# Weight panels loaded as two half transfers, each with its own semaphore

## The reference

```python
z = jnp.einsum("bsd,de->bse", n, w_in.astype(n.dtype))              # first block: mixer in
...
q = jnp.einsum("td,de->te", xt, w_q.astype(xt.dtype))               # expert router
u = expert_u[idx]
v = expert_v[idx]                                                    # 16 of 16384 experts per head and token
act = jax.nn.gelu(jnp.einsum("thkd,td->thk", u, xt))
return jnp.einsum("thk,thkd->td", (gate * act).astype(v.dtype), v)
...
def swiglu(h, w_gate, w_up, w_down):                                 # second block, four times
    return (jax.nn.silu(h @ w_gate) * (h @ w_up)) @ w_down
```

## Time and profile before

| | |
|---|---|
| time, median of 3 runs | 4292.24 us (4284.7 to 4296.47) |
| the profiled execution: its time | 4296.63 us |
| the profiled execution: its span | 4294.8 us |
| mean granted TensorE clock | 0.933 |
| PE busy | 3777.9 us, 88% of the span |
| POOL busy | 1952.1 us, 45% |
| ACT busy | 1503.3 us, 35% |
| DVE busy | 2245.2 us, 52% |
| moved by the DMA engines | 570.20 MB, mean 133 GB/s |

### The profile page before, as it was taken

How to read it: one execution, slowest core, us unless ns; L and a number is a source line. 1 busy time by engine, 2 the same in 40 slices (tenths; PEclk the granted TensorE clock), 3 DMA queues, 4 the chain that set the end, 5 groups by cost and what they waited for, 6 DMA issues and landing times. The chain is left out here.

```text
span 4294.8 us, 51143 instructions
## 1 busy us (share of the span) xinstructions
PE 3777.9 (88%) x17668; PEld 3146.6 (73%) x17668; DVE 2245.2 (52%) x3388; ACT 1503.3 (35%) x2617; POOL 1952.1 (45%) x1517
## 2 busy tenths in 40 slices
PE   6948998997888889999989884999979998469999
PEld 5526888997888889988867722788758886247887
DVE  4662696884899976663326225433243321544330
ACT  3222444663222233354322312343234422233432
POOL 3724565335666667755533300444435543004444
PEclk9978999998999999999999966999989999579999
DMA  3002344457999979733332200232313335002322
GB/s 117 15 25 83 113 157 139 147 196 283 344 334 337 338 283 352 283 98 98 93 122 62 78 0 0 85 96 91 91 59 98 97 94 106 33 1 85 97 90 91
DMA packets 172780, 570.20 MB, mean 133 GB/s; under 512 B 15457, under 2 KB 58593, under 8 KB 155140
## 3 DMA queue, kind: packets, MB, share of 16 engines
q1 hardware_dynamic: 152244, 427.68, 30.6%
q0 software_dynamic: 20432, 141.31, 9.0%
HBM read 518.85 MB, written 50.07 MB: 132 GB/s over the span
## 5 line engine op out<-in xcount | busy, mean ns | idle before, releaser
L262 POOL TENSOR_TENSOR weight_low<-weight_ring,weight_high 128x512 fp32r<-128x512 f32 x1264 | 1720.1, 1372 | 1906.1 <-ACT weight_high L234 1032.8
L277 PE MATMUL banks<-normed_high,weight_high 128*128 128x512 f32 (+1 forms) x2592 | 973.1, 375 | 118.4 <-POOL weight_low L262 115.3
L278 PE MATMUL banks<-normed_low,weight_high 128*128 128x512 f32 (+1 forms) x2592 | 962.8, 371 | 0.0
L279 PE MATMUL banks<-normed_high,weight_low 128*128 128x512 f32 (+1 forms) x2592 | 962.1, 371 | 0.0
L277 PEld LDWEIGHTS banks<-normed_high,weight_high 128*128 128x128 f32 x2592 | 494.2, 191 | 203.5 <-POOL weight_low L262 136.9
L236 ACT ACTIVATE weight_high<-weight_ring 128x512 fp32r<-128x512 f32 (+1 forms) x632 | 389.6, 616 | 673.9 <-PE banks L279 673.9
L234 ACT ACTIVATE weight_high<-weight_ring 128x512 fp32r<-128x512 f32 x632 | 398.5, 631 | 612.6 <-PE banks L279 511.4
L278 PEld LDWEIGHTS banks<-normed_low,weight_high 128*128 128x128 f32 x2592 | 494.3, 191 | 62.9 <-issue 0.5
L279 PEld LDWEIGHTS banks<-normed_high,weight_low 128*128 128x128 f32 x2592 | 493.4, 190 | 62.7
L277 PE MATMUL banks<-parked_high,weight_high 128*128 128x384 f32 x768 | 271.4, 353 | 58.6 <-POOL weight_low L262 32.3
L1733 DVE TENSOR_TENSOR square<-square,banks 128x512 f32<-128x512 f32 x88 | 60.6, 688 | 416.7 <-PE banks L279 415.9
(11 more groups left out here) (364 smaller groups left out, 6022.9 us busy)
## 6 DMA issues: line engine op xcount, KB each, us to landing
weight_ring<-in_experts SPq DMA_DIRECT2D x256, 512.0 KB
weight_ring<-in_ffn_gate SPq DMA_DIRECT2D x88, 512.0 KB
weight_ring<-in_ffn_up SPq DMA_DIRECT2D x88, 512.0 KB
weight_ring<-in_ffn_down SPq DMA_DIRECT2D x64, 512.0 KB
expert_gates<-spread_space SPq DMA_DIRECT2D x6, 4096.0 KB, 12.2
parked_space<-expert_gates SPq DMA_DIRECT2D x24, 768.0 KB
parked_space<-parked_activations SPq DMA_DIRECT2D x24, 768.0 KB
weight_ring<-in_a_w_in SPq DMA_DIRECT2D x28, 512.0 KB
```

The lines of the kernel that those rows point to most:

```text
L262: m.nc.gpsimd.tensor_tensor(m.w_lo[:, s % PARTS, at], m.ring[:, s, at], m.w_hi[:, s % PARTS, at].bitcast(FP), ALU.subtract).then_inc(done, 1)
L277: m.nc.tensor.matmul(out, w_hi, hi(c), start=(first and c == 0), stop=False)
L278: m.nc.tensor.matmul(out, w_hi, lo(c), start=False, stop=False)
L279: ins = m.nc.tensor.matmul(out, w_lo, hi(c), start=False, stop=(last and c == chunks - 1))
```

## The change

The load of a panel becomes two transfers. The first brings columns 0 to 511 of each partition (chunks 0 to 3) and counts a new semaphore `half_loaded[s]`. The second brings the rest and counts `loaded[s]`. ACT's first activation waits for `half_loaded[s]`, its second one for `loaded[s]` and, as before, for `used`. A partition's piece in either transfer is 2 KB (1 KB in the second half of the six-chunk panels), where it was 4 KB (3 KB).

```diff
+        self.half_loaded = [self.sem(f"panel_half_loaded{s}") for s in range(SLOTS)]
         self.loaded = [self.sem(f"panel_loaded{s}") for s in range(SLOTS)]
...
     sp.wait_ge(m.low, low_count(p - SLOTS))
-    sp.dma_start(m.ring[:, s, 0:width], source).then_inc(m.loaded[s], 16)
+    sp.dma_start(m.ring[:, s, 0:HALF], source[:, 0:HALF]).then_inc(m.half_loaded[s], 16)
+    sp.dma_start(m.ring[:, s, HALF:width], source[:, HALF:width]).then_inc(m.loaded[s], 16)
 
 
 def split_high(m, act, p, s, width=PANEL):
 
     turn, k = p
-    act.wait_ge(m.loaded[s], turn * 16 + 16)
+    act.wait_ge(m.half_loaded[s], turn * 16 + 16)
 
     act.wait_ge(m.half_used, turn * SLOTS + used_count(k - PARTS))
     m.nc.scalar.activation(m.w_hi[:, s % PARTS, 0:HALF], m.ring[:, s, 0:HALF], ACT.Copy).then_inc(m.half_high, 1)
+    act.wait_ge(m.loaded[s], turn * 16 + 16)
     act.wait_ge(m.used, turn * SLOTS + used_count(k - PARTS))
     m.nc.scalar.activation(m.w_hi[:, s % PARTS, HALF:width], m.ring[:, s, HALF:width], ACT.Copy).then_inc(m.high, 1)
```

## The result

The changed kernel takes 4305.94 us, median of 11 runs (4302.02 to 4309.72), beside 4297.3 us for the kernel before on the same chip. The ratio is 1.0023, 95% interval 1.0014 to 1.0032, which is 9.9 us more (6.0 to 13.7); the two medians differ by 8.6. The forecast was 4293 us, +1 on the median of three runs that was known then (4292.24), with a range from 4279 to 4309. So the time lies in the range and within 0.3% of before. Of the 12.9 us that it lies above the forecast, 5.1 are the median of the kernel before, which is 4297.3 with eight more runs. Of the difference that the change makes, nine tenths were not in the sum. The profiled execution has a span of 4303.3 us. The added lines shift the numbering by one to three (L225 is now L226 and L227, L234 and L236 are L236 and L239, L262 is L265).

A forecast was written before the change was run, and what follows sets the result against it. The prediction took PE as the bound, busy 3777.9 of 4294.8 us, with weight panels mostly landing well ahead. Terms +1 + 3 - 1 - 2 = +1 us on 4292.24 gave 4293 us, range 4279 to 4309.

The forecast's parts named there:

- SP's second issue: On SP, 632 more issues of 333 ns, 210 us, covered by its wait for POOL: cost 0.
- ACT's second wait: On ACT, 68 ns for each of 632 panels, covered by its wait for PE: 0, bounds 0 and +19 us.
- The same bytes in smaller pieces: Weight loads in 2 KB pieces cost little more, mattering only near DMA's limit in the experts: +1 us, up to +10.
- the share within 0.02 of 0.94: Sign in the experts: DMA share stays within 0.02 of 0.94; 0.98 or more would prove the prediction wrong.
- The dilated block: Dilated layer's first block: 2 KB weight pieces alternate with the bias-line store, a panel takes 13.3 us, not 7.46: +3 us.
- the case in which this term would have been 0: Dilated layer's first block: two 2 KB pieces share a packet, so its term is 0 and the sum -2.
- The branch that I named for that case: Dilated layer's first block: if the store lands no sooner, the same count gives +4.5 us.
- First halves that land sooner: ACT's waits of 3.7 us on `experts` and `b_w_out` shrink by up to half: -1 us, bounds 0 and -2.
- Picked rows: POOL's row fetches, which DVE awaits, wait less behind smaller weight pieces: -2 us, bounds 0 and -15.
- the rival at 4280: Experts: halving the weights' turn favours the late gates and picked rows; 4280 us at its upper bound, chance 0.10.
- The rival of a fixed cost per transfer: Experts: engines held for each transfer's fixed 1.2 us, deciding from 0.3 us on; about 4433 us, chance 0.03.
- The rival of SP held at the issue: SP held at issues delays gates' fetches: +15 to +20, 4310 us; chance 0.10 together with piece costs.

## Why the prediction was right, and where not

*SP's second issue and ACT's second wait, cost 0.* Right. PE is busy for 50.00 of 50 us in the feed-forward, ACT waits for no `in_ffn` panel, and SP's wait for POOL has given up 300 us (200 were forecast). The two were not tried apart from the second transfer.

*The same bytes in smaller pieces, +1, bounds 0 to +10.* The term was mis-sized, and it was about the wrong thing. In the dense experts it measured +6.3 us over three groups in this pair, 8.4 in the mean of all traces. Two transfers without smaller pieces cost it all; pieces alone may have a part. The step that failed is the count: I counted rows and left out the second transfer itself, with its 16 semaphore pieces and whatever goes with its end. The bound that I set, the share within 0.02 of 0.94, held at 0.92 while the stage lost 2.9%: the share hardly saw it, the GB/s did (343 to 334 over the three groups).

*The dilated block, +3, bounds 0 to +4.5.* The alternation was right and the size was off: +4.9, above the bound too. I divided 7.46 us by 8 rows and got 0.93, where there are 9 pieces of 0.83. I then split the turn in 0.74 us for the store and the weight row's own 0.19, where the store alone has a turn of 0.80 and the row adds 0.03. Two 2 KB pieces did not share a turn, the case in which this term would have been 0. My 0.83 us for a 2 KB piece was then right by luck, 16 of them make the 13.3, and the two semaphore pieces make the 14.7. The second error follows from the same split: that the store would land 3.4 us sooner with less weight traffic between its pieces. It landed 0.8 us sooner, for its turns were hardly shorter; its own pieces took longer, 764 ns in the median over the whole store instead of 721. With 54.0 to 55.2 us it lands at nearly the same time in every kernel with 128 copies, even with rows of 1 KB. The branch that I named for that case, +4.5, was the one that happened.

*First halves that land sooner, -1.* Not there. The wait on `experts` is 3.4 instead of 3.8 us, the first of the program 10.2 instead of 9.9, and ACT's wait before the block's end is 3.93, on `b_w_q`, instead of 3.71.

*Picked rows, -2, and with it the rival at 4280.* The gain didn't come: 60.4 us in 35 waits, not 49.8 in 29. That it's a loss is likely and not certain, since with only the experts in halves it was 48.9 us and with halves and the short store 54.0, against 47.9 to 52.7 us in the traces with whole panels there. Smaller turns for the weights were to favour the fetches, but the GB/s in the stage fell.

*The rival of a fixed cost per transfer, 0.03.* Its mechanism is the nearest to what the experts show, at 0.17 us instead of 1.2. I took it to bite only beyond 0.28 us, the mean slack of a panel. That was wrong. That picked rows and gates come in bursts, so that the mean slack doesn't count, is my reading and wasn't tested. The fit of 2.0 us that the prediction took for it from the Trainium skill, page "DMA: Bandwidth & Descriptors", stands there in the section "Anatomy of one DMA — SWDGE (gpsimd) path", for transfers that GpSimd issues, and not in the section on rules; the panels are SP's, and no term rested on it.

*The rival of SP held at the issue.* SP is indeed held, up to 5.0 us where 3.6 was the longest. In the dilated block before, only one of the four issues from 3597.14 on was held for long (3.0 us); in the changed kernel nine in a row from 3601.31 on took 4.4 to 5.0 us each. It cost nothing there, for the halves landed 7.36 us apart and the issues stayed ahead of them. In the experts single second issues take up to 1.1 us; whether these belong to the 0.17 us, no run has separated.

In sum, +8 for the experts and +5 for the dilated block stand against +9.9 (6.0 to 13.7) measured; the forecast had +1 - 2 - 1 and +3 for the same places. It stayed in the range because its bounds had been kept wide there (0 to +10, 0 to +4.5). That the reason for the wide bound in the experts, slower small rows, was not the main cost makes this luck in part.

What stays open: where the 0.17 us of a transfer goes, between its last row and the next transfer's first on an engine, or in SP's issue, and how much of the experts' loss smaller pieces have. Nor is it known why the weights stay off the store's engines for the first 18 us. The price of ACT's two waits apart from the two transfers wasn't tried. Nor was a store laid out so that all 16 engines carry it.

## What to carry to other kernels

A transfer that is cut in two has a price even if the bytes and the rows stay the same: count its transfers and the semaphore pieces beside the rows, above all where a second stream runs on the same engines. Before loads are cut finer, look at who waits for them: 8 of 632 panels here, and in the one stretch where they were late they were behind another transfer, which was the thing to shorten. Read GB/s beside the DMA share, since the share went from 0.92 to 0.91 while the throughput fell by 2.6%, and with confined transfers the share rose to 1.01 while a fifth of it went.

## What the runs showed of the hardware

- Between two streams on a DMA engine the turn goes by pieces, whatever they hold: 4096, 2048, 1024 or 4 bytes each waited for one 5120-byte piece of the store, 0.81 to 0.83 us a turn, where the store alone has a turn of 0.80.
- A transfer ends with one 4-byte piece on each of 16 engines (10112 more for 632 more transfers). 9 ns long by itself, it takes a full turn of 0.8 us beside the store.
- The store of 12 heads ran on 12 of the 16 engines: a quarter of each load, 32 rows and 4 semaphore pieces, passed the other four at once.
- Loads confined to partitions 0 to 63 or 64 to 127 moved 270 GB/s at a share of 1.01, where even and odd partitions moved 340 at 0.93. A 4 KB piece took 255 ns instead of 159.
- Reads into 16 partitions had 4 KB pieces of 566 ns, reads into 64 partitions 308, and reads into 128 partitions 159. Eight of the first side by side landed after 18.7 us (median).
- An issue on SP that takes 0.33 us mostly was held for 4.4 to 5.0 us nine times in a row with halves beside the store, and once for 24.8 us with 1 KB pieces.
- 256 transfers of 64 bytes from DRAM to DRAM cost 29.6 us in stages with a DMA share above 0.9, 0.40 us each in the three groups, where the pieces beside them were slower too.
